# Modulation rows of a streaming encoder: partial rows turned by TensorE transposes and summed by VectorE, the identity matrix with a signal of its own, small loads issued behind the conditioning's activation

## The reference

```
def ada_modulation(c, w, b):
    mod = jax.nn.silu(c) @ w + b                  # (9, 2048) @ (2048, 12288), once per layer
    return [m[:, None, :] for m in jnp.split(mod, N_MOD, axis=-1)]

for i in range(DEPTH):
    shift1, scale1, gate1, shift2, scale2, gate2 = ada_modulation(c, w_ada[i], b_ada[i])
    h = rms_norm(x, g_mix[i]) * (1.0 + scale1) + shift1
    mix = attention(h) if i == 0 else pool_mixer(h)
    x = x + gate1 * mix
    h = rms_norm(x, g_ffn[i]) * (1.0 + scale2) + shift2
    x = x + gate2 * (silu(h @ w_gate) * (h @ w_up)) @ w_down
```

## Time and profile before

| | us |
|---|---|
| median of 3 runs | 3439.44 |
| lowest and highest | 3436.16, 3441.07 |
| the profiled execution, its own time | 3440.21 |
| its span (first to last instruction) | 3438.4 |

### The profile page before, as it was taken

The page is one execution under the profiler, slowest core; times in us unless marked ns, Lnnn a source line. Parts: engine busy times, 40 slices in busy tenths (PEclk is TensorE's granted clock), DMA queues, the critical chain, the costliest instruction groups (busy, mean ns, idle before and its releaser), DMA issues.

```text
span 3438.4 us, 48286 instructions
## 1 busy us (share of the span) xinstructions
PE 3290.4 (96%) x20405; PEld 2983.9 (87%) x20405; DVE 2095.9 (61%) x1804; ACT 1309.0 (38%) x991; POOL 140.6 (4%) x141
## 2 busy tenths in 40 slices
PE   7999998889989999999999999769999999999999
PEld 4677776667979999999999999659999999999999
DVE  3487885556887667676776767685444443334443
ACT  3344444455453443334433343334222232232221
POOL 0000000000000000000000000010000000000000
PEclk9999999999989999999999999889999999999999
DMA  9777767877645655556555555553433433333331
GB/s 353 272 259 241 246 241 250 294 273 262 221 166 175 208 203 180 186 183 209 194 178 188 195 203 187 181 187 134 130 126 122 130 126 122 131 125 122 124 132 62
DMA packets 325817, 646.50 MB, mean 188 GB/s; under 512 B 10882, under 2 KB 13514, under 8 KB 325322
## 3 DMA queue, kind: packets, MB, share of 16 engines
q1 hardware_dynamic: 317144, 630.17, 53.6%
q10 hardware_dynamic: 8586, 15.09, 1.2%
HBM read 631.46 MB, written 14.74 MB: 188 GB/s over the span
## 4 chain that ended last, share of the span: by engine, by line
PE 87%; DVE 5%; DMA 4%; ACT 3%; issue 1%; POOL 0%; SPq 0%; ACTq 0%; DVEq 0%; POOLq 0%
PE bank L1501 23%; PE bank L1503 23%; PE bank L1502 23%; PE bank L1583 3%; PE bank L1528 3%; PE bank L1584 3%; PE bank L1585 3%; DMA raw<-in_w_ada 3%; PE bank L1688 1%; PE bank L1537 1%; PE bank L1513 1%; PE bank L1716 1%; DMA raw<-in_cache_k 0%; PE bank L1717 0%; DVE w_lo L955 0%
## 5 line engine op out<-in xcount | busy, mean ns | idle before, releaser
L955 DVE TENSOR_TENSOR w_lo<-raw,w_hi 128x2048 fp32r<-128x2048 f32 x323 | 739.1, 2291 | 901.5 <-ACT w_hi L578 901.5
L578 ACT ACTIVATE w_hi<-raw 128x2048 fp32r<-128x2048 f32 x323 | 616.1, 1914 | 1373.3 <-PE bank L1503 1180.3
L1501 PE MATMUL bank<-h_hi,w_hi 128*128 128x384 f32 x3136 | 1064.1, 339 | 31.9 <-DVE h_lo L1034 24.0
L1502 PE MATMUL bank<-h_lo,w_hi 128*128 128x384 f32 x3136 | 1052.4, 336 | 0.0
L1503 PE MATMUL bank<-h_hi,w_lo 128*128 128x384 f32 x3120 | 1048.0, 336 | 0.0
L1501 PEld LDWEIGHTS bank<-h_hi,w_hi 128*128 128x128 f32 x3136 | 592.2, 189 | 77.1 <-issue 68.7
L1502 PEld LDWEIGHTS bank<-h_lo,w_hi 128*128 128x128 f32 x3136 | 592.4, 189 | 0.0
L1503 PEld LDWEIGHTS bank<-h_hi,w_lo 128*128 128x128 f32 x3120 | 589.0, 189 | 0.0
L1501 PE MATMUL bank<-act_hi,w_hi 128*128 128x384 f32 x1408 | 473.0, 336 | 0.0
L1503 PE MATMUL bank<-act_hi,w_lo 128*128 128x384 f32 x1408 | 470.5, 334 | 0.0
L1502 PE MATMUL bank<-act_lo,w_hi 128*128 128x384 f32 x1408 | 470.5, 334 | 0.0
(11 more groups left out here) (226 smaller groups left out, 2530.6 us busy)
## 6 DMA issues: line engine op xcount, KB each, us to landing
raw<-in_w_ada SPq DMA_DIRECT2D x192, 1024.0 KB, 5.9
raw<-in_w_gate SPq DMA_DIRECT2D x88, 1024.0 KB, 5.2
raw<-in_w_up SPq DMA_DIRECT2D x88, 1024.0 KB, 5.2
raw<-in_w_down SPq DMA_DIRECT2D x88, 1024.0 KB, 5.1
raw<-in_w_qkv SPq DMA_DIRECT2D x40, 1024.0 KB, 5.2
raw<-in_cache_k SPq DMA_DIRECT2D x32, 1024.0 KB, 6.3
raw<-in_cache_v SPq DMA_DIRECT2D x32, 1024.0 KB, 7.8
raw<-in_w_o SPq DMA_DIRECT2D x15, 1024.0 KB, 5.1
```

What stands on the lines that cost most here:

```text
L578: act.activation(w_hi[:, s], raw[:, s], ACT.Copy).then_inc(hi_ready, 1)
L955: dve.tensor_tensor(w_lo[:, s], raw[:, s], w_hi[:, s].bitcast(f32), ALU.subtract).then_inc(lo_ready, 1)
L1501: pe.matmul(out, w, a, start=start, stop=False)
L1502: pe.matmul(out, w, al, start=False, stop=False)
```

## The change

Six edits.

- `ada_turn`: the four matmuls with `fold` or `fold3` become four transposes of the quarters of `mod` against `ident`. They write all 512 columns of the bank instead of 36.
- `mod_in`: VectorE first sums the partial rows out of the bank (`tensor_reduce`: 36 results from 144 elements per partition with `pieces=1`, from 432 with `pieces=3`), waits for its own result, and then adds the bias. `pieces=1` is used for the opening's 8 blocks and the mixer's 4, `pieces=3` for the other 36.
- `fold` and `fold3` are gone, with their 18 instructions on GpSimd.
- `ident_ready`: GpSimd signals behind the identity; TensorE's first transposes wait for that, and for `const_ready` only behind the first block.
- ScalarE waits for `crow` and applies Silu ahead of its nine small load issues instead of behind them.
- VectorE's arithmetic on `icount` moves behind the split of `c`.

```diff
@@ mod_in
-                dve.tensor_tensor(modA[:, m, :],
-                                  bank[:, t_bank, 0:4 * NC].rearrange("p (k c) -> p k c", k=4),
-                                  bias, ALU.add).then_inc(ada_done, 1)
+                parts = bank[:, t_bank, :].rearrange("p (m j q) -> p m j q", m=4, j=4)[:, :, :, 0:pieces * NC]
+                if pieces == 1:
+                    step.mark(dve.tensor_reduce(modA[:, m, :], parts.rearrange("p m j c -> p m c j"), AX.X, ALU.add))
+                else:
+                    step.mark(dve.tensor_reduce(modA[:, m, :], parts.rearrange("p m j (r c) -> p m c j r", r=pieces), AX.XY, ALU.add))
+                own()
+                dve.tensor_tensor(modA[:, m, :], modA[:, m, :], bias, ALU.add).then_inc(ada_done, 1)
@@ ada_turn
-                    last = pe.matmul(bank[:, t_bank, t * NC:(t + 1) * NC], mod[:, t * P:(t + 1) * P], weights[:], start=True, stop=True)
+                    last = pe.transpose(bank[:, t_bank, t * P:(t + 1) * P], mod[:, t * P:(t + 1) * P], ident[:])
@@ GpSimd
+            pool.memset(tmp_s[:, 0, 4:5], 0.0).then_inc(ident_ready, 1)
...
-            do(pool.memset(fold[:], 0.0))
-            do(pool.memset(fold3[:], 0.0))
-            for j in range(4):
-                do(pool.affine_select(out=fold[:], ...
-                for r in range(3):
-                    do(pool.affine_select(out=fold3[:], ...
@@ ScalarE (the two lines stood behind the small loads)
+            act.wait_ge(c_loaded, 32)
+            act.activation(csil[:], crow[:], ACT.Silu).then_inc(silu_c, 1)
             for i in range(2):
                 act.dma_start(prow[:, i], b_ada[i]...
@@ TensorE, start
-            pe.wait_ge(const_ready, 1)
+            pe.wait_ge(ident_ready, 1)
             pe.wait_ge(silu_c, 1)
...
             ada_block(0, 6, first=True)
+            pe.wait_ge(const_ready, 1)
             pe.wait_ge(par_loaded, 16 * 7)
```

More of the change, by code:

```diff
@@ L149, in encoder_step @@
         mask, _ = nxt("mask", [P, 512])
-        fold, _ = nxt("fold", [P, NC])
-        fold3, _ = nxt("fold3", [P, NC])
         mod, _ = nxt("mod", [P, 512])
@@ L212, in encoder_step @@
         hi_ready, lo_ready, sub_used = sem("hi_ready"), sem("lo_ready"), sem("sub_used")
-        pool_step, const_ready = sem("pool_step"), sem("const_ready")
+        pool_step, const_ready, ident_ready = sem("pool_step"), sem("const_ready"), sem("ident_ready")
         x_loaded, c_loaded, par_loaded = sem("x_loaded"), sem("c_loaded"), sem("par_loaded")
@@ L522, in _ @@
                                   pattern=[[-STEP, STREAMS], [0, STEP]], channel_multiplier=1))
-            do(pool.memset(fold[:], 0.0))
-            do(pool.memset(fold3[:], 0.0))
-            for j in range(4):
-                do(pool.affine_select(out=fold[:], in_=fold[:], compare_op=ALU.not_equal, fill=1.0,
-                                      base=-C32 * j, pattern=[[-1, NC]], channel_multiplier=1))
-                for r in range(3):
-                    do(pool.affine_select(out=fold3[:], in_=fold3[:], compare_op=ALU.not_equal, fill=1.0,
-                                          base=-(C32 * j + NC * r), pattern=[[-1, NC]], channel_multiplier=1))
             for i in range(4):
@@ L664, in _ @@
                 act.dma_start(gqk[:, i], g[0:1, :].to_broadcast([P, HD])).then_inc(gqk_loaded, 16)
-            act.wait_ge(c_loaded, 32)
-            act.activation(csil[:], crow[:], ACT.Silu).then_inc(silu_c, 1)
             act.wait_ge(x_loaded, 16 * TT)
@@ L975, in dense, with mod_in @@
                 lo(W, [s])
-            def mod_in(a, t_bank, part=None):
+            def mod_in(a, t_bank, part=None, pieces=3):
                 m = ds(4 * (a if part is None else part), 4)
                 dve.wait_ge(ada_t, a + 1)
+                parts = bank[:, t_bank, :].rearrange("p (m j q) -> p m j q", m=4, j=4)[:, :, :, 0:pieces * NC]
[4 more added lines that the diff above has]
+                own()
                 bias = par[:, m].unsqueeze(2).to_broadcast([P, 4, NC])
-                dve.tensor_tensor(modA[:, m, :],
-                                  bank[:, t_bank, 0:4 * NC].rearrange("p (k c) -> p k c", k=4),
-                                  bias, ALU.add).then_inc(ada_done, 1)
+                dve.tensor_tensor(modA[:, m, :], modA[:, m, :], bias, ALU.add).then_inc(ada_done, 1)
             def norm_coef(n, k0=0, tiles=KT):
@@ L1086, in _ @@
             dve.memset(c32[:], 0.0).then_inc(c32_ready, 1)
[L1087 to L1091, removed]
             dve.wait_ge(cT_done, 1)
@@ L1097, in _ @@
             c_pieces()
+            dve.wait_ge(const_ready, 1)
+            for i, w in enumerate(WINDOWS):
+                step.mark(dve.tensor_scalar(icount[:, i], icount[:, i], float(w), None, ALU.min))
+            own()
+            step.mark(dve.reciprocal(icount[:], icount[:]))
             for t in range(TT):
@@ L1115, in _ @@
             dve.wait_ge(par_ready, 1)
-            mod_in(0, 7, FIRST[0])
+            mod_in(0, 7, FIRST[0], 1)
             dve.wait_ge(rs_done, 1)
@@ L1122, in _ @@
                 if g:
-                    mod_in(i, 7, FIRST[i]); early(i)
-                mod_in(i + 1, 7, FIRST[i + 1])
+                    mod_in(i, 7, FIRST[i], 1); early(i)
+                mod_in(i + 1, 7, FIRST[i + 1], 1)
                 norm_coef(0, 4 * g, 4)
@@ L1413, in dense_chunk @@
                         rows_out(s)
-            with loop(dve, 0, CHUNKS - 1, {step: 4 * ADD}) as c:
+            with loop(dve, 0, CHUNKS - 1, {step: 4 * ADD + 2}) as c:
                 mixed_chunk(W_FFN0 + c * 5, c, ADA_FFN + c * 2, 0, R_FFN0 + c * 4, mixed)
@@ L1479, in _ @@
                 if j % 2:
-                    mod_in(ADA_POOL + j // 2, 3)
+                    mod_in(ADA_POOL + j // 2, 3, pieces=1)
                 if j >= 3 and j % 2:
@@ L1529, in ada_sub, with ada_turn @@
                 last.then_inc(sub_used, 1)
-            def ada_turn(a, t_bank, weights=fold3):
+            def ada_turn(a, t_bank):
                 pe.wait_ge(mod_ready, a + 1)
@@ L1611, in _ @@
             pe.wait_ge(par_ready, 1)
-            ada_turn(0, 7, fold)
+            ada_turn(0, 7)
             pe.wait_ge(xT_dve, 6)
@@ L1619, in _ @@
             ada_block(1, 6)
-            ada_turn(1, 7, fold)
+            ada_turn(1, 7)
             def early(d, turn=None):
@@ L1628, in early @@
                     if k == 2 and turn is not None:
-                        ada_turn(turn, 7, fold)
+                        ada_turn(turn, 7)
                     kt = 4 * j + k
@@ L1941, in _ @@
                 if j % 2:
-                    ada_turn(ADA_POOL + j // 2, 3, fold)
+                    ada_turn(ADA_POOL + j // 2, 3)
                 elif j:
```

## The result

The changed kernel took **3421.55 us** (median of 5 runs, 3420.2 to 3424.23) against 3439.44 for the kernel before (5 runs beside it, 3433.68 to 3441.37): a ratio of 0.9952, 95% interval 0.9937 to 0.9966, 17.9 us less. The forecast was 3428.0, with a range from 3424. The direction and the price of a turn were right; 6.4 us of gain (17.9 less the forecast 11.5) were not foreseen.

A forecast was written before the change was run, and what follows sets the result against it. TensorE, busy 96% of the span, was taken as the bound, with VectorE at 61%. Terms -13.0 + 0.2 + 0.3 + 1.0 = -11.5 us from 3440.2 gave 3428.7, less 0.8 for the median: 3428, range 3424 to 3435.

The forecast's parts named there:

- The turn on TensorE: 34 turns in TensorE's full stream: four transposes take 0.44 us in place of 0.79 or 0.89, saving 13.0 us together.
- The second bound, 0.59 from attention: Turn priced by attention's four transposes, 0.59 us near a wait for ScalarE; the 34 turns would then save only 7.9 us.
- Rival 2: Transposes need two passes like fold matmuls, 0.87 us a turn; kernel at 3442 us; chance 8%.
- The sum on VectorE: `mod_in` grows by 0.34 us with `pieces=1`, 0.64 with `pieces=3`; mostly off the path, so nothing counted outside named places.
- the cover of 1.5 us: At an FFN chunk's second turn, the reduction delays TensorE only if it takes over 1.5 us.
- The tenth turn: Stands alone behind Q, K and V; attention's first bank waits for its `mod_in`: -0.48 + 0.64 = +0.2 us.
- the opening's last sum: Opening's last `mod_in`, directly ahead of scaling the last quarter of `h`, for which TensorE waits: +0.3 us.
- the mixer: VectorE carries the path there; three of four longer `mod_in` on the path, +1.0 us (0 to 1.4).
- The start: Opening's earlier Silu and transposes gain 0, all spent waiting for the second quarter's weights.
- Rival 4: Transposes make TensorE's clock fall after each of 34 turns, costing 70 us, 3500; chance 2%.
- 2 us either way: Allowance in the forecast's own bounds for the median of a new set of runs.
- 7.9 on TensorE and 1.9 on VectorE: Ends of the forecast's own bounds: TensorE gain 7.9 to 13.0 us, VectorE's places 0.2 to 1.9 us.

The follow-up runs named there:

- e7: The changed kernel with each turn done twice, eight transposes over each other: 3440.93 us, ratio 1.0010 to the kernel before.
- e8: The changed kernel with the 36 reductions of 432 elements done three times, two of them into a spare tile: 3421.4 us, ratio 0.9955.
- e12: The changed kernel with the fold matmul kept for the mixer's four turns and the opening's last one: 3417.58 us, ratio 0.9948.
- e3: The kernel before with only the opening's edits (`ident_ready`, earlier Silu, later `icount`), turns by fold as before: 3436.59 us, ratio 0.9999.
- e6: The kernel before with the opening's edits, turns by fold, plus 56 tiny transposes at TensorE's start: 3437.3 us, ratio 0.9996.
- e10: The kernel before with 56 tiny transposes in front of TensorE's first ones, nothing else changed: 3436.44 us, ratio 0.9999.
- e5: The changed kernel with 72 tiny transposes added at TensorE's start: 3427.65 us, ratio 0.9965 to the kernel before.
- e14: The changed kernel with a tiny transpose (9 x 128) behind each of a turn's four: 3465.06 us, ratio 1.0078 to the kernel before.
- e15: The changed kernel with 72 tiny transposes at TensorE's start, a repeat of an earlier padding run: 3426.64 us, ratio 0.9965.
- e2: The changed kernel, unchanged, timed and profiled again: 3417.61 us (6 runs), ratio 0.9947 to the kernel before.
- e9: The changed kernel with 36 tiny transposes in front of TensorE's first ones: 3421.44 us, ratio 0.9957 to the kernel before.
- e13: The kernel before with two of each turn's four fold matmuls, half of the modulation left out: 3422.08 us, ratio 0.9952.

## Why the prediction was right in kind and too small

- **The turn on TensorE: right.** 0.44 us forecast and read; 0.35 saved ahead of `ada_sub` (0.39 measured), 0.45 between products (0.79 + 0.28 - 0.44 - 0.18). The sum of 34 turns was 13.0 forecast, 13.6 measured. The second bound, 0.59 from attention, was the wrong neighbour: e7's pure run of eight has 0.109 each. Rival 2 falls by the same row.
- **The sum on VectorE: right.** 0.30 and 0.60 us, and the cover of 1.5 us confirmed by e8. The Trainium skill's formula (VectorE: DVE Perf Modes, "The TRN2 errata") gives an estimated 0.58; the trace has 0.60.
- **The tenth turn +0.2** (0.24 measured), **the opening's last sum +0.3** (0.34 from the reduction's start to the sum's; the stage's 0.38 is one execution), **the mixer +1.0** (0.85 by the stages, 1.2 against e12): right.
- **The start, 0: right.** The wait moved from 1.91 to 4.28 us in front of the second quarter and the fourth quarter's start stayed; e3 gives 0.9999 (+-0.0009).
- **Rival 4, the clock: no fall behind a turn.** The first FFN with its 22 turns has a granted clock of 1.00 throughout, the 2.4 GHz level.
- **The step that failed** is the sentence under the range that outside the named places only "2 us either way" could differ. The terms' sum was good to 0.6 us (11.5 forecast, 12.1 read); 17.4 +- 1.1 was measured by means. The 5.3 left lie where the change has no term, and the larger part is TensorE's clock: the kernel before loses 62.7 us to it, the changed kernel 59.0, which is 3.7 +- 1.1 us. Not every such us lengthens a launch; over the 81 executions of the kernel before the span moves by 0.76 us for each, so the clock's part is 2.8 to 3.7 us. What remains is 1.6 to 2.5, no more than twice its error. TensorE's stall in attention fits it (2.80 us before, 0.23 after; it moves with the number of instructions ahead: gone or at most 0.50 in e6 and e10, back in e5, e7, e14 and e15). The prediction asked only whether the transposes would make the clock fall, never what the stretches at the 1.2 GHz level that the kernel already had were worth. An execution has such a stretch or has not, behind the same wait. For `w_lo` in Q, K and V the kernel before waits 2.57 us and has one, the changed kernel's first profile waits 2.60 and has none, its second (e2) waits 2.60 and has one again (windows of before, after and e2; the clock is third from the end):

```profile
176.00:184.00 8.00, 7.77 (x21) 6.14 (x22) 7.16 (x5) 2.74 (x2) 0.00 (x0) 0.60 0.90 303
```
```profile
172.00:180.00 8.00, 5.40 (x33) 3.74 (x32) 7.16 (x5) 3.73 (x2) 0.00 (x0) 1.00 0.64 212
172.00:180.00 8.00, 5.47 (x18) 4.37 (x19) 7.15 (x5) 3.71 (x2) 0.00 (x0) 0.79 0.80 255
```

So that stretch, most of the 2.3 us between the sums 7 and 8 in the table above, was the luck of one profiled execution. The prediction's own bounds also hold a slip without effect: 7.9 on TensorE and 1.9 on VectorE, with 2 us either way, end at 3435, not at 3434.

**What stays open.** That the stall is a wait for code is well supported (14 of 14 end behind an instruction packet), and so is that its place follows the code. Its worth isn't shown: attention's length follows the clock and hardly the stall, the paddings of the kernel before gave back 2.0 +- 0.8 and 0.9 +- 1.0 us by mean spans (e10, e6), and e9 had a stall for free. The padding of the changed kernel cost 6 us twice; 4.7 of them are time lost to the clock (63.7 against 59.0 us). Why the clock is lower in one kernel than in another isn't known. The length of the code alone doesn't set it: e13 has the changed kernel's number of instructions and loses 63.6 us. Nor was any run able to say what decides whether the clock falls behind a given wait.

## What to carry to other kernels

Price a change of instruction by a row with the same neighbours, and it can be right to half a microsecond. Outside the named places a kernel isn't fixed. Two things differed here from variant to variant: stretches of TensorE at the lower clock, 3.7 us between the two kernels, and the places where an engine with a long unrolled stream waits for its code (idle time that ends in "issue", up to 2.8 us each). List both in the profile of before, compare mean clocks over many executions and not in one profile, and widen the range by them. Where VectorE carries the path keep the fold (e12, by its stages), where TensorE is full use the transposes.

## What the runs showed of the hardware

- Four fp32 matmuls with 9 moving columns (0.79 us) cost more than four fp32 transposes with 128 (0.44): a matmul is two passes of 0.10 us, a transpose one of 0.109.
- A transpose of 9 rows behind one of 128 is dear: the pair takes 0.42 us (e14), two of the large ones 0.22.
- TensorE can wait up to 2.8 us where the profile names no releaser, and each such wait ended 1.27 to 1.52 us behind a 16 KB instruction packet. All lie in attention, a stretch that changes between many short code blocks; in the FFN's loop, whose code repeats, no profile shows one.
- The same wait of 2.6 us is followed by a fall to the 1.2 GHz level in one execution and not in another, and the kernels' mean clocks of 0.98177 and 0.98273 over 81 and 11 executions are 3.7 us of lost time apart.
